# A mixture-of-experts decoder step: filler rows dropped from gathers and scatters, second expert weight laid out by pairs of rows

## The reference

```python
logits = xf @ w_router + b_router
top_v, top_i = lax.top_k(logits, 4)
gates = softmax(top_v)
# for each expert e, over the tokens that chose it:
h = xb @ w1[e] + b1[e]                    # 1024 -> 2048
x_glu = minimum(h[:, 0::2], 7.0)
x_lin = clip(h[:, 1::2], -7.0, 7.0)
a = x_glu * sigmoid(1.702 * x_glu) * (x_lin + 1.0)
y = a @ w2[e] + b2[e]                     # 1024 -> 1024
out[token] += y * gate
```

## Time and profile before

| | us |
|---|---|
| median of 3 runs | 1615.84 (1608.74 to 1617.58) |
| the profiled execution | 1619.37 |
| its span, first to last instruction | 1617.5 |
| busy in the span: PE | 1448.4 (90%) |
| VectorE | 439.0 (27%) |
| GpSimd | 340.1 (21%) |
| ScalarE | 219.3 (14%) |
| DMA read from DRAM | 442.74 MB |

### The profile page before, as it was taken

How to read it: one execution, slowest core, us unless ns; L and a number is a source line. 1 busy time by engine, 2 the same in 40 slices (tenths; PEclk the granted TensorE clock), 3 DMA queues, 4 the chain that set the end, 5 groups by cost and what they waited for, 6 DMA issues and landing times.

```text
span 1617.5 us, 33932 instructions
## 1 busy us (share of the span) xinstructions
PE 1448.4 (90%) x13508; PEld 721.7 (45%) x13508; DVE 439.0 (27%) x1023; ACT 219.3 (14%) x524; POOL 340.1 (21%) x338
## 2 busy tenths in 40 slices
PE   7999997998869998999899899799989989989981
PEld 6778876774542433333243343233324334334330
DVE  2212534434553221212121122121212112212125
ACT  0003000333000111101111111110111111111010
POOL 5322201001231212121122122212112312221112
PEclk9999996558877999999999999999999999999995
DMA  9244002204036899999999999999999999999963
GB/s 304 44 88 113 27 27 89 79 1 173 14 131 253 312 405 394 409 394 402 406 393 392 405 391 405 395 390 395 402 404 382 394 403 391 406 397 401 403 233 114
DMA packets 127025, 467.50 MB, mean 289 GB/s; under 512 B 31382, under 2 KB 51962, under 8 KB 94096
## 3 DMA queue, kind: packets, MB, share of 16 engines
q1 hardware_dynamic: 98704, 425.45, 66.3%
q0 software_dynamic: 27440, 37.20, 10.0%
q10 hardware_dynamic: 736, 2.65, 0.4%
HBM read 442.74 MB, written 23.42 MB: 288 GB/s over the span
## 4 chain that ended last, share of the span: by engine, by line
PE 42%; DMA 12%; DVE 7%; SPq 5%; issue 3%; POOLq 0%; ACT 0%; POOL 0%; DVEq 0%
PE PS L1340 24%; PE PS L1362 15%; DMA ring<-in_w_moe_dram 12%; SPq L477 4%; DVE mix L1879 2%; DVE qmT L1884 1%; DVE qmT L1886 1%; PE PS L1353 1%; PE PS L1332 1%; DVE qmT L1883 1%; DVE qmT L1880 1%; SPq L473 1%; PE PS L1322 1%; DVE ring L1942 0%; DVE ring L1940 0%
## 5 line engine op out<-in xcount | busy, mean ns | idle before, releaser
L1340 PE MATMUL PS<-ring,mix 128*32 128x512 f32 x5632 | 635.3, 604 | 53.2 <-issue 31.0
L1340 PEld LDWEIGHTS PS<-ring,mix 128*32 128x32 f32 x5632 | 181.3, 111 | 466.6 <-issue 411.6
L757 POOL DMA_INDIRECT expert_rows<-mix,smalls x88 | 140.0, 1590 | 805.4 <-issue 496.8
L1879 DVE TENSOR_TENSOR mix<-PS,kn 128x512 f32<-128x512 f32 x88 | 60.9, 691 | 656.2 <-PE PS L1340 650.0
L1362 PE MATMUL PS<-ring,mix 128*32 128x256 f32 x3584 | 201.7, 380 | 0.0
L1362 PEld LDWEIGHTS PS<-ring,mix 128*32 128x32 f32 x3584 | 112.4, 110 | 76.8 <-issue 5.4
L748 POOL DMA_INDIRECT mix<-x_rows,smalls x88 | 87.4, 993 | 66.5 <-issue 57.7
L927 ACT COPY mix<-PS 128x512 f32<-128x512 f32 (+1 forms) x48 | 25.0, 553 | 528.2 <-PE PS L1332 528.2
L1025 PE MATMUL PS<-xT,ring 128*128 128x280 f32 x384 | 96.5, 414 | 0.0
L1013 PE MATMUL PS<-ring,xT 128*128 128x256 f32 (+1 forms) x400 | 94.5, 399 | 1.3 <-issue 1.1
L1025 PEld LDWEIGHTS PS<-xT,ring 128*128 128x128 f32 x384 | 75.5, 198 | 22.0 <-issue 1.9
(11 more groups left out here) (370 smaller groups left out, 1073.6 us busy)
## 6 DMA issues: line engine op xcount, KB each, us to landing
ring<-in_w_moe_dram SPq DMA_DIRECT2D x320, 1024.0 KB, 19.9
xT<-in_w_moe_dram SPq DMA_DIRECT2D x32, 1024.0 KB, 24.0
X<-in_w_moe_dram SPq DMA_DIRECT2D x32, 1024.0 KB, 24.5
ring<-in_w_in_dram SPq DMA_DIRECT2D x9, 1024.0 KB, 18.3
ring<-in_w_out_dram SPq DMA_DIRECT2D x4, 1024.0 KB, 10.4
expert_rows<-X ACTq DMA_DIRECT2D x5, 512.0 KB
X<-in_x_prompt_dram SPq DMA_DIRECT2D x4, 512.0 KB, 6.0
ring<-in_state_mlstm_C_dram POOLq DMA_DIRECT2D x1, 2048.0 KB, 16.2
```

Source lines behind the costliest of these rows:

```text
L757: nc.gpsimd.indirect_dma_start(out=y_blocks, out_offset=bass.IndirectOffsetOnAxis(ap=lists[a][:, g, 1:2].bitcast(U32), axis=0), in_=ysb[g] ...
L1340: ins = mm(bank(BANK0[a] + g)[32 * t:32 * t + 32, :], xgT[XBUF[a][g]][:, P * (k % 2) + 32 * (k // 2):P * (k % 2) + 32 * (k // 2) + 32], sl ...
L1879: link(V.tensor_tensor(ht, bank(BANK0[a] + g), b1b, ALU.add))
```

## The change

Three things change. The tile `blank` now holds 2,080 (4 x 520) in both index words, one past the last quarter row, so the iota on GpSimd goes; gathers and scatters carry a bound of 2,079 with errors off, so that a filler place is out of bounds and is skipped. With that `expert_rows` loses its 128 additional rows, ACT's sixth write goes, and the waits on `y_set` count five writes. A skipped place of a gather keeps what an earlier group left in the tile; its result has gate 0 and is not written.

A W2 chunk is laid out so that partition p has rows 2p and 2p + 1 of the 256, one run of 8 KB. The activations must match: transpose u takes the columns u, u + 2, u + 4, ... of `lt` instead of 128 neighbouring ones. The memory set on GpSimd of a small constant tile goes through the same helper as its neighbours, with the same semaphore count.

```diff
--- before.py
+++ after.py
@@ -216,7 +216,7 @@
                   consts, rel_consts,
                   y_prompt, y_sample, kp_out, vp_out, Cp_out, np_out, mp_out, ks_out, vs_out, Cs_out, ns_out, ms_out):
     x1_dram = nc.dram_tensor("x1_rows", (NTOK, D), F32).ap()
-    y_dram = nc.dram_tensor("expert_rows", (NTOK + P, D), F32).ap()
+    y_dram = nc.dram_tensor("expert_rows", (NTOK, D), F32).ap()
     table = nc.dram_tensor("token_lists", (E, 32, LISTG, 4), F32).ap()
     band_dram = nc.dram_tensor("relative_bias_band", (HA, P, 2 * P), F32).ap()
 
@@ -475,7 +475,7 @@
                 else:
                     d = c - 8
                     sp.dma_start(rowpair(s), w2[0, bass.ds(e, 1), 2 * P * d:2 * P * d + 2 * P, :].rearrange(
-                        "e (k p) n -> p (e k) n", p=P)).then_inc(slot_in[s], 16)
+                        "e (p k) n -> p (e k) n", k=2)).then_inc(slot_in[s], 16)
 
             def load_bias(e):
                 sp.dma_start(b1q[0:P:32, :], b1[0, bass.ds(e, 1), :].rearrange("e (t n) -> t (e n)", t=4)).then_inc(b1_in, 16)
@@ -559,7 +559,7 @@
             second = expert_at(1)
             for c in range(2):
                 load_chunk(second, 8 + c, W2[1][c])
-            sp.wait_ge(y_set, 16 * (NT + 2))
+            sp.wait_ge(y_set, 16 * (NT + 1))
             for c in range(2, 4):
                 load_chunk(second, 8 + c, W2[1][c])
             for k in range(EARLY[0]):
@@ -620,9 +620,7 @@
 
             for i in range(4 * PRIME):
                 dma(prime[0:1, i:i + 1], consts[0:1, 0:1]).then_inc(y_out[i % 4], 16)
-            pool.wait_ge(zeroed, 2)
-            link(nc.gpsimd.iota(blank[:, :, 1], [[0, LISTG // 4], [P, 4]], base=4 * NTOK, channel_multiplier=4,
-                                allow_small_or_imprecise_dtypes=True))
+            pool.wait_ge(zeroed, 3)
             dma(table.rearrange("e i g w -> i e (g w)"),
                 blank.rearrange("p g w -> p (g w)").unsqueeze(1).to_broadcast([32, E, 4 * LISTG])).then_inc(table_set, 16)
             dma(rel_c, rel_consts).then_inc(rel_in, 16)
@@ -691,8 +689,7 @@
 
             dma(lng, bass.AP(ln1_g.tensor, 0, [[0, P], [1, D]])).then_inc(ln_in, 16)
             dma(lnb, bass.AP(ln1_b.tensor, 0, [[0, P], [1, D]])).then_inc(ln_in, 16)
-            nc.gpsimd.memset(powc, -0.5).then_inc(pool_chain, 1)
-            link.count[pool_chain.name] += 1
+            link(nc.gpsimd.memset(powc, -0.5), wait=False)
             nc.gpsimd.iota(iota, [[1, E]], base=0, channel_multiplier=0, allow_small_or_imprecise_dtypes=True)
             nc.gpsimd.iota(tokid, [[P, NT + 1]], base=0, channel_multiplier=1,
                            allow_small_or_imprecise_dtypes=True).then_inc(iota_done, 1)
@@ -746,7 +743,7 @@
                 for g in range(GROUPS[a]):
                     i = XBUF[a][g]
                     nc.gpsimd.indirect_dma_start(out=xg[i], out_offset=None, in_=x1_blocks, in_offset=bass.IndirectOffsetOnAxis(
-                        ap=lists[a][:, g, 0:1].bitcast(U32), axis=0)).then_inc(xg_in[i], 16)
+                        ap=lists[a][:, g, 0:1].bitcast(U32), axis=0), bounds_check=4 * NTOK - 1, oob_is_err=False).then_inc(xg_in[i], 16)
 
             def scatter(group, a, g, earlier):
                 pool.wait_ge(y_done, group + (g + 3))
@@ -756,12 +753,12 @@
                 pool.sem_inc(steps, 1)
                 nc.gpsimd.indirect_dma_start(out=y_blocks, out_offset=bass.IndirectOffsetOnAxis(
                     ap=lists[a][:, g, 1:2].bitcast(U32), axis=0), in_=ysb[g], in_offset=None,
-                    compute_op=ALU.add).then_inc(y_out[g], 16)
+                    compute_op=ALU.add, bounds_check=4 * NTOK - 1, oob_is_err=False).then_inc(y_out[g], 16)
 
             pool.wait_ge(x1_out, 16 * (NT + 1))
             gather(0, None, 0)
             gather(1, None, 1)
-            pool.wait_ge(y_set, 16 * (NT + 2))
+            pool.wait_ge(y_set, 16 * (NT + 1))
 
             def expert_rows(j, a):
                 n = j * ROUND + a
@@ -960,7 +957,6 @@
                 r = NS if small(tt) else P
                 act.wait_ge(y_ready, tt + 1)
                 act.dma_start(y_dram[P * tt:P * tt + r, :], X[0:r, tt, :]).then_inc(y_set, 16)
-            act.dma_start(y_dram[NTOK:NTOK + P, :], X[:, 0, :]).then_inc(y_set, 16)
             with act.Fori(0, ROUNDS - 1) as j:
                 for a in range(ROUND):
                     expert(j, a)
@@ -1350,7 +1346,7 @@
                 if g >= 2:
                     pe.wait_ge(turn_ready, group + (g - 1))
                 for u in range(2):
-                    ins = tr(bank(6 + g % 2)[:, P * u:P * u + P], lt[g % 2][:, P * u:P * u + P], ident)
+                    ins = tr(bank(6 + g % 2)[:, P * u:P * u + P], lt[g % 2][:, u::2], ident)
                 ins.then_inc(turn_mm, 1)
 
             def second_product(a, group, g, slots, arrived):
@@ -1427,7 +1423,8 @@
             V = nc.vector
             link = Chain(dve, dve_chain)
             V.memset(X[0:64, NT, :], 0.0).then_inc(zeroed, 1)
-            V.memset(blank, 0.0).then_inc(zeroed, 1)
+            V.memset(blank[:, :, 2:4], 0.0).then_inc(zeroed, 1)
+            V.memset(blank[:, :, 0:2], 4.0 * NTOK).then_inc(zeroed, 1)
             for c in range(4):
                 V.memset(cadd[32 * c:32 * c + 32, :], float(c))
             V.memset(wgp, 0.0)
```

## The result

The changed kernel takes 1590.52 us (median of 4 runs, 1586.88 to 1595.56) against 1615.01 of the kernel before, timed beside it (4 runs, 1608.74 to 1617.58): ratio 0.9856, 95% interval 0.9816 to 0.9896. The forecast was 1595 in a range of 1585 to 1611, and the forecast of "faster" holds.

What follows compares the result with a forecast made beforehand. PE's own work was taken as the floor, about 21 us below the present time. DMA work falls 26.6 + 6 = 33 us, giving back 20 us of chunk waits plus 1 for the earlier start: 1595 us, range 1585 to 1611.

Steps and rivals of the forecast that it cites:

- The main step: Expert stage: PE is the floor; a faster DMA gives back some 19 to 21 of 21.3 us of chunk waits.
- The filler term: Gathers and scatters on the software queue: skipping the 26.1% filler rows takes 26.6 us off DMA work, at least zero.
- What was expected of the packets: Software queue, 600 to 1,500 us: packets fall from 14,170 by about a quarter, its share from 9.5% to 7.0%.
- the third rival: Gathers and scatters: a skipped row saves nothing, total 1612 us, shown if the software queue's packets stay; chance 0.13.
- The pair term: W2 chunks as one 8 KB run per partition: 6 us less DMA work, between 0 and 7.
- The strided load: The 176 transposes at L1353 loading alternate columns: taken as zero cost, at most 34 us.
- The first rival: Jump of PE's loop: the issue gap is partly a chunk wait, 1 us off each of six; 1586 us, chance 0.14.
- The second rival: Slowest DMA engine decides, so the filler saving is 11 us, not 26.6; 1605 us, chance 0.17.
- The fourth: Strided weight load slows the 176 transposes, deciding from 121 ns each, at most 193; 1629 us, chance 0.08.
- The check of bounds: Gathers and scatters on POOL: no issue cost; any would hide in POOL's 805.4 us of idle before L757.
- The write that went: ACT's write at L963: its removal starts the second expert's remaining W2 chunks 1 to 2 us earlier.
- SP's waits: Weight-load queue's waits for PE to free slots: rise by about as much as DMA work falls.

Runs made afterwards that it cites:

- e1: Changed kernel with only the filler skipping kept, second weight in the old layout and contiguous transposes: 1597.8 us, ratio 0.9882 to the kernel before.
- e2: Kernel before with only the second weight by pairs of rows and transposes by alternate columns, fillers still moved: 1605.73 us, ratio 0.9937.
- g1: Kernel before with PE's loop over rounds written out as straight code, nothing of the change: 1609.52 us, ratio 0.9963.
- f1: Changed kernel with PE's loop over rounds written out as straight code: 1585.3 us, ratio 0.9819 to the kernel before.
- f2: Changed kernel with contiguous transposes, the step of two moved to VectorE's (lt + 1) * gt and ScalarE's sigmoid reads: 1589.15 us, ratio 0.9844 to the kernel before.
- g4: Changed kernel with the step of two in VectorE's product and ScalarE's sigmoid, and PE's loop written out: 1586.84 us, ratio 0.9824 to the kernel before.
- e3: Changed kernel with contiguous transposes, VectorE's two clamps reading with a step of four instead: 1595.86 us, ratio 0.9871 to the kernel before.
- g2: Changed kernel with only the filler skipping kept, old second-weight layout, contiguous transposes, PE's loop written out: 1596.33 us, ratio 0.9892 to the kernel before.
- f4: Changed kernel with 48 unread PE operations ahead of its first transpose, operands at steps of 1 to 4: one run, 1601.81 us.

## Why the prediction was right, and which of its steps were not

**The main step held.** PE was taken as the floor, 21.3 us above it as waits for chunks, and all of them as what a faster DMA side gives back. They went whole; e1 and e2 show that either part alone leaves 7 to 9 us. The stage's idle time fell by 25.7 us (74.2 to 48.5, from 1074.6 less 1000.4 and 1055.1 less 1006.6): chunk waits 21.3, issue 1.3, the wait for VectorE 1.2, and 1.7 for ScalarE's turned activations (L1362 before). Busy time rose by 6.3. That the total comes within 5 us of the forecast is in part luck: some 4 us of other waits and 2.6 us behind the stage came on top of the 21, PE's longer busy time took about as much away, and neither was in the sum.

**The filler term was too large.** 26.6 us were counted from a share of 9.5% times 26.1%. The share fell to 7.5%, 18 us of the 900, or 21 scaled by 88 to 75, nearly as the prediction did. Between 600 and 1500 us only 24% of the scatters' rows are filler, a skipped row keeps its packet of 9 ns, and the scatters' packets that stay take 2 ns longer; these make up most of the difference. What was expected of the packets (a quarter fewer) was wrong, and by the prediction's own test that spoke for the third rival. The test was a bad one: the count stayed at some 14,300 and the bytes fell from 19.12 to 14.43 MB. e1 refutes that rival outright: 18 us faster than the kernel before, timed beside it (1616.21), by the fillers alone.

**The pair term was too small as DMA work.** Three windows of 4 and 8 us, 411 against 419 GB/s, gave 6 us. The hardware queue from 600 to 1500 us (92.7% for 337.35 MB before; 92.8% for 342.61 after) took 2.473 us per MB and takes 2.438: 0.035 on 403 MB of weights are 14 us. The packets say nearly the same: before, one of 8 KB takes 317.8 ns and two of 4 KB 329.2, which for 16,384 of them over 16 engines is 12 us. The term rested on a difference of 2% between short windows. Both errors nearly cancel: 33 us of DMA work were forecast, and 21 + 14 came out by the rows. Only 24.2 of them show as time with the loop written out (16.6 for the fillers and 7.3 for the pairs by the stages). Even there transfers don't set the pace all the time, since SP still waits 174 us (g1) and 203 us (f1) for PE at its second-weight slots; whether that is the whole reason no run shows.

**The strided load was not free.** The zero for 176 loads is 66 ns each in the records and 7.4 us in the transposes (37.2 to 44.6). L1099, the row that I went by, was 64 by 8, too small to tell. Every load shows the step's price (194 ns at least), but little of it reaches the total: f2 takes the step away and gains 3.5 us in the stage, but L1336 alone is 3.9 us shorter there, by the clock; and g4 against f1 gains nothing. So no run shows a price in the total that stands clear of the clock. In the prediction's sum it would have been a few us against the 21; it did not change the outcome. The Trainium skill, "SBUF — State Buffer", says in its text on cachelines that reads keep full rate while two or more fall in one 16-byte line. For TensorE's load of weights these traces disagree (140 to 206, and 162 to 200 ns at a step of two). VectorE's reads agree with it: a step of two costs it nothing (425 ns packed, 426 in f2), and a step of four, one value to a line, costs 36 to 41% (401 and 417 ns against 294 and 295, e3).

**The first rival was nearly false as it stood, and true in another way.** The six gaps are 4.8 to 5.1 us, and the chain at the one shown has no transfer ahead of it. Before, five of the six were 4.8 to 5.1 too, and one was 6.2; e1 and e2 have such long ones as well (up to 6.2 and 6.0 us), the kernels with no chunk waits left have none. So part of a single gap, 1.1 us or so, may have been a wait for a chunk, not 1 us of each. But f1 and g1 show that the DMA side uses them: a gap gone is a wait for a chunk come. **The second rival** is not settled by name. Its test was 8 us of chunk waits with a quarter fewer packets; with the pairs in, none were left, and e1's 8.5 us lie at its edge. The queue's bytes fell by 25% and its share by 21%; that share is a mean over 16 engines and can't tell how the relief is spread. The time can, in part: the rival gives the fillers 11 us of DMA work, and g2 is 13.2 us below g1 in the median and 16.6 in the stage. That speaks against its size, but no view names a packet's engine. **The fourth** has its mechanism (66 ns) but not its size (121 ns to decide).

**Smaller terms.** The check of bounds costs POOL 54 ns a gather (992 to 1046), not nothing, and L754's 785.9 us of idle hide it, as foreseen. The write that went lets SP's load follow the stage's start by 7.3 us (508.47 after 501.2) in place of 8.6 (515.52 after 506.9): 1.3 us, about the 1.5 expected. What I missed is the end. With scatters skipping fillers the part behind the stage takes 33.7 to 34.2 us in all nine kernels, and 36.3 or 36.4 in the four without. In the final norm VectorE's wait of 1.7 us for POOL is gone, and its wait to read `expert_rows` back falls from 20.0 to 17.8 us.

**SP's waits** were to rise by about what the DMA work falls, some 33 us. They rose by 265 (58.9 + 208.2 before at these two lines, 532.1 after). While the DMA side was behind, SP stood in the hand-over of the loads and not at a semaphore, and that time shows in no wait: between 600 and 1500 us its issues of weight loads (L473, L477) take 420 us before and 177 after, where the shortest of them takes 0.33. A queue's waits say that there is slack, not how much.

## What to carry to other kernels

Where PE and DMA are both near full, read the waits for transfers as about the most that lighter transfers can give, and take the edits together: the second one finds less to shorten. Before removing a stop of the busy engine, ask what the other side does in it; here 30 us of stops were worth 3 to 7 us. A layout that makes the runs of a transfer longer moves a step into an on-chip access and is paid there. Here a step of two in TensorE's load and one in VectorE's and ScalarE's reads came out alike in the total; a step of four in VectorE's reads made the stage 4.2 us longer, and scattered writes 10.1.

## What the runs showed of the hardware that I had not expected

- A row left out by the bounds check of an indirect transfer still makes a packet: 8 bytes and 9 ns for a scattered row of 1 KB that took 102 ns, 16 bytes and 11 ns for four gathered rows that took 160. The queue keeps its packet count and loses bytes and time (9.5 to 7.5% of the engines). The scatters that add gain more than twice what the gathers do (1.4 and 0.6 points).
- TensorE's load of 128 columns in f32 takes 140 ns packed and 206 with a step of two in the expert stage; steps of 2, 3 and 4 cost alike (200, 196, 208 against 162, f4). A moving operand of 128 columns costs nothing more at a step of two and some 110 to 135 ns a record at a step of four (f4).
- A DMA packet of 8 KB takes 318 ns of an engine, two of 4 KB 329 (kernel before).
- On VectorE 256 values in f32 take 295 ns with reads 8 bytes apart, 401 and 417 with reads 16 bytes apart, and 432 and 440 with writes 512 bytes apart.
- Six jumps of PE's loop cost 5 us each and a granted clock of 0.97 in place of 1.00 in a round's mean. Straight code of eight rounds showed no fetch gap of its own (0.3 us of issue at L1336).
- The start of the expert stage moved by 8 us between kernels that are all but alike up to there; I did not find what moves it.
